# Attention by pairs of heads, first table rows beside the scores, values ahead of the gates in the combining

## The reference, cut to what matters

```python
def softmax_attend(q, k, v):
    s = jnp.einsum('bqhd,bkhd->bhqk', q, k).astype(jnp.float32) * MLA_SCALE
    p = jax.nn.softmax(s, axis=-1).astype(v.dtype)
    return jnp.einsum('bhqk,bkhd->bqhd', p, v)
...
def peer_ffn(h, wq, k1, k2, u, v):
    ...
    s1 = jnp.einsum('thd,kd->thk', q[..., :PEER_HALF], k1).astype(jnp.float32)
    s2 = jnp.einsum('thd,kd->thk', q[..., PEER_HALF:], k2).astype(jnp.float32)
    t1, i1 = lax.top_k(s1, PEER_TOPK)
    t2, i2 = lax.top_k(s2, PEER_TOPK)
    ...
        ue = jnp.take(u, ib, axis=0)
        ve = jnp.take(v, ib, axis=0)
        act = jax.nn.gelu(jnp.einsum('td,thkd->thk', hb, ue), approximate=False)
        return jnp.einsum('thk,thkd->td', gb * act, ve)
```

## Time and profile before

| | us |
|---|---|
| median of three executions (4664.24 to 4667.33) | 4665.28 |
| the profiled execution's own time | 4668.22 |
| its span, first to last instruction | 4666.4 |
| TensorE busy | 4111.4 (88%) |
| VectorE busy | 2964.6 (64%) |
| ScalarE busy | 1555.0 (33%) |
| GpSimd busy | 1471.2 (32%) |
| bytes moved | 1004.75 MB, 215 GB/s |

### The profile page before, as it was taken

How to read it: one execution, slowest core, us unless ns; L and a number is a source line. 1 busy time by engine, 2 the same in 40 slices (tenths; PEclk the granted TensorE clock), 3 DMA queues, 4 the chain that set the end, 5 groups by cost and what they waited for, 6 DMA issues and landing times. The chain is left out here.

```text
span 4666.4 us, 71661 instructions
## 1 busy us (share of the span) xinstructions
PE 4111.4 (88%) x23812; PEld 2234.3 (48%) x23812; DVE 2964.6 (64%) x8223; ACT 1555.0 (33%) x1960; POOL 1471.2 (32%) x1087
## 2 busy tenths in 40 slices
PE   5999779789999999699999996887888887789996
PEld 1556565556565566344444441443445454534442
DVE  2025544244664664688888886584188888688887
ACT  0014321024444444322222221681045443433332
POOL 0500000321111111166666650210512332277774
PEclk8989989899999999899999998898989998999998
DMA  5100221256877877699999984211388999999996
GB/s 213 58 24 4 75 73 72 82 133 165 242 196 186 235 190 200 211 370 338 350 338 350 339 310 167 77 59 59 109 226 265 338 314 323 326 337 344 345 343 226
DMA packets 374788, 1004.75 MB, mean 215 GB/s; under 512 B 35024, under 2 KB 121872, under 8 KB 367248
## 3 DMA queue, kind: packets, MB, share of 16 engines
q1 hardware_dynamic: 208188, 522.43, 32.4%
q0 software_dynamic: 101376, 318.81, 24.1%
q10 hardware_dynamic: 64996, 160.55, 9.2%
HBM read 804.43 MB, written 146.90 MB: 204 GB/s over the span
## 5 line engine op out<-in xcount | busy, mean ns | idle before, releaser
L1368 PE MATMUL ca_A<-hh,ca_uh 128*128 128x512 f16 (+2 forms) x3072 | 797.3, 314 | 135.1 <-DMA ca_ul<-ca_ur 72.2
L1368 PE MATMUL ca_A<-hl,ca_uh 128*128 128x512 f16 (+2 forms) x3072 | 796.9, 314 | 0.0
L1368 PE MATMUL ca_A<-hh,ca_ul 128*128 128x512 f16 (+2 forms) x3072 | 795.7, 314 | 0.0
L1332 POOL DMA_DIRECT2D ca_ul<-ca_ur x192 | 170.4, 887 | 1171.2 <-ACT ca_ul L1401 1109.7
L1874 PE MATMUL ex_R<-ex_vh,ex_wh 128*128 128x512 f16 x1280 | 486.4, 380 | 29.2 <-DVE ex_wl L1888 29.2
L1874 PE MATMUL ex_R<-ex_vl,ex_wh 128*128 128x512 f16 x1280 | 486.4, 380 | 0.0
L1874 PE MATMUL ex_R<-ex_vh,ex_wl 128*128 128x512 f16 x1280 | 486.1, 380 | 0.0
L1368 PEld LDWEIGHTS ca_A<-hh,ca_uh 128*128 128x128 f16 x3072 | 261.9, 99 | 329.7 <-issue 86.9
L1409 ACT ACTIVATE ca_ga<-ca_A 128x640 f32<-128x640 f32 (+1 forms) x256 | 152.7, 596 | 673.1 <-PE ca_A L1368 606.5
L1368 PEld LDWEIGHTS ca_A<-hh,ca_ul 128*128 128x128 f16 x3072 | 262.3, 99 | 196.5 <-issue 15.1
L1368 PEld LDWEIGHTS ca_A<-hl,ca_uh 128*128 128x128 f16 x3072 | 262.0, 99 | 190.8 <-issue 14.0
(11 more groups left out here) (374 smaller groups left out, 7767.5 us busy)
## 6 DMA issues: line engine op xcount, KB each, us to landing
ca_ur<-in_peer_u SPq DMA_DIRECT2D x256, 512.0 KB, 5.2
ex_vr<-in_peer_v SPq DMA_DIRECT2D x256, 512.0 KB, 7.5
gates<-ca_stage ACTq DMA_DIRECT2D x32, 2048.0 KB, 11.7
ca_ul<-ca_ur POOLq DMA_DIRECT2D x192, 256.0 KB, 5.2
acts<-ca_ga ACTq DMA_DIRECT2D x128, 320.0 KB, 2.6
ex_gr<-gates SPq DMA_DIRECT2D x32, 1280.0 KB, 7.8
ex_ar<-acts SPq DMA_DIRECT2D x128, 320.0 KB, 4.9
acts<-ca_ga ACTq DMA_DIRECT2D x128, 192.0 KB, 6.1
```

The lines of the kernel that those rows point to most:

```text
L1332: nc.gpsimd.dma_start(ul[j][:, :, :].rearrange("p k n -> p (k n)"), ur[j][:, :, :].rearrange("p k n -> p (k n)"), accum_op=ALU.add).then_i ...
L1368: last = nc.tensor.matmul(A[b][:, a:a + w], lhs[j][:, k, :], rhs[:, k, a:a + w], start=(k == 0 and x == 0), stop=(k == KD - 1 and x == 2))
```

## The change

In attention, the head's weights shrink to 3 x 128 columns for the queries and 2 x 64 for the keys; the values' weights of all heads are a tensor of their own, loaded once, and one token tile's values are made for all eight heads at once (two products of 512 columns, two tiles behind each of the first three pairs of heads). The keys of two heads are made by turns into rows 0 to 63 and 64 to 127 of `at_T`. The steps are numbered by pairs (`place`): two steps that follow are the two heads of a pair at the same tile. Their second products are made together, one step later than before, by turns into the two halves of one output; the copies of probabilities have four buffers, two of them in the space of the rotary turning, so ScalarE waits for `roped` first. VectorE copies the output of both at once, every second step.

The ring of the choosing, its semaphores among them, is made before the scores (`table_ring`) and cleared with a barrier behind the choosing. In the scores SyncE loads its first four chunks after all weights, and VectorE makes their high and low parts ahead of the last two score copies (`first_cut`). The choosing then begins with chunk 4 in its refills, and ScalarE, VectorE and GpSimd leave out their work on the first four chunks.

In both combining stages SyncE loads the four values of the first group first, then gates, then activations; ScalarE casts the values first; VectorE makes the first group's low parts of the values ahead of the weights; and GpSimd starts with the gathers. The second layer's (`combine_with_dots`) is changed as the first's, which is shown.

```diff
+        w = [sb(f"at_w{j}", [P, W_Q + W_K]) for j in range(2)]
+        wv = sb("at_wv", [P, 2, HEADS * V_DIM])
...
-        probT = [sb(f"at_pT{j}", [P, TOK]) for j in range(2)]
+        probT = [sb(f"at_pT{j}", [P, TOK]) for j in range(2)] + [rot[:, j, :] for j in range(2)]
...
-        C = ps("at_C", [P, TILES, V_DIM])
-        O0 = ps("at_O", [P, P])
-        O = (O0[0:64, :], C[0:64, 0:2, :].rearrange("p a d -> p (a d)"))
+        C = [ps(f"at_C{j}", [P, HEADS * V_DIM]) for j in range(2)]
+        O = [x[:, 0:P] for x in C]
...
+            def place(n):
+                m, s = divmod(n, 2)
+                g, i = divmod(m, TILES)
+                return 2 * g + s, i
+
+            keys = lambda n: CTX if place(n)[1] < CTX_TILES else TOK
...
+                    sp.dma_start(w[0][:, :], io["ev_w_up"][0]).then_inc(w_in[0], 16)
+                    sp.dma_start(w[1][:, :], io["ev_w_up"][1]).then_inc(w_in[1], 16)
                     sp.dma_start(cs[64:128, :], io["rope"]).then_inc(cs_in, 16)
-                    for h in range(1, HEADS):
-                        if h >= 2:
-                            sp.wait_ge(v_done, h - 1)
-                        sp.dma_start(w[h % 2][:, :, :], io["ev_w_up"][h].rearrange("p (k m) -> p k m", k=5)).then_inc(w_in[h % 2], 16)
+                    sp.dma_start(wv[:, :, :], io["ev_w_up_v"]).then_inc(wv_in, 16)
+                    for g in range(1, PAIRS):
+                        sp.wait_ge(k_done, g)
+                        for s in range(2):
+                            sp.dma_start(w[s][:, :], io["ev_w_up"][2 * g + s]).then_inc(w_in[s], 16)
...
+                    def key_pair(g):
+                        if g >= 1:
+                            pe.wait_ge(k_copied, 2 * g)
                         for a, n in HALVES:
                             for kk in range(2):
-                                last = nc.tensor.matmul(T[0:64, a:a + n], w[j][:, 3 + kk, 0:64], PT[:, C_KV + kk, a:a + n],
-                                                        start=(kk == 0), stop=(kk == 1))
+                                for s in range(2):
...
+                                    last = nc.tensor.matmul(T[64 * s:64 * s + 64, a:a + n], w[s][:, W_Q + kk * NOPE:W_Q + kk * NOPE + NOPE],
+                                                            PT[:, C_KV + kk, a:a + n], start=(kk == 0), stop=(kk == 1))
                         last.then_inc(k_done, 1)
...
+                    def values(t):
+                        if t >= 2:
+                            pe.wait_ge(v_copied, t - 1)
+                        for kk in range(2):
+                            last = nc.tensor.matmul(C[t % 2][:, :], PT[:, C_KV + kk, t * P:t * P + P], wv[:, kk, :],
+                                                    start=(kk == 0), stop=(kk == 1))
                         last.then_inc(v_done, 1)
...
+                    def mix_values(m):
+                        pe.wait_ge(pt_copied, 2 * m + 2)
+                        if m >= 2:
+                            pe.wait_ge(out_copied, m - 1)
+                        blocks = keys(2 * m) // P
+                        for b in range(blocks):
+                            for s in range(2):
+                                h, i = place(2 * m + s)
+                                last = nc.tensor.matmul(O[m % 2][64 * s:64 * s + 64, :], v[:, h, b, :],
+                                                        probT[(2 * m + s) % 4][:, b * P:b * P + P], start=(b == 0), stop=(b == blocks - 1))
+                        last.then_inc(av_done, 1)
+
+                    for g in range(PAIRS):
+                        queries(2 * g)
+                        queries(2 * g + 1)
+                        key_pair(g)
+                        if g == 0:
+                            pe.wait_ge(wv_in, 16)
+                        for t in range(2 * g, min(2 * g + 2, TILES)):
+                            values(t)
+                    pe.wait_ge(q_copied, HEADS)
+                    pe.wait_ge(k_copied, HEADS)
+                    pe.wait_ge(roped, HEADS)
+                    scores(0)
+                    scores(1)
+                    pe.wait_ge(v_copied, TILES)
+                    for n in range(STEPS):
+                        turn(n)
                         if n + 2 < STEPS:
                             scores(n + 2)
-                        pe.wait_ge(pt_copied, n + 1)
-                        if n >= 2:
-                            pe.wait_ge(out_copied, n - 1)
-                        for b in range(keys(n) // P):
-                            last = nc.tensor.matmul(O[n % 2], v[:, h, b, :], probT[n % 2][:, b * P:b * P + P],
-                                                    start=(b == 0), stop=(b == keys(n) // P - 1))
-                        last.then_inc(av_done, 1)
+                        if n >= 2 and n % 2 == 0:
+                            mix_values(n // 2 - 1)
+                    mix_values(STEPS // 2 - 1)
...
+                    for g in range(PAIRS):
+                        for s in range(2):
+                            h = 2 * g + s
+                            act.wait_ge(q_done, h + 1)
+                            nc.scalar.activation(q[0:64, h, :], A[s][0:64, 0:TOK], ACT.Copy).then_inc(q_copied, 1)
+                        act.wait_ge(k_done, g + 1)
+                        for s in range(2):
+                            nc.scalar.activation(k[2 * g + s][0:64, :], T[64 * s:64 * s + 64, 0:TOK], ACT.Copy).then_inc(k_copied, 1)
+                        for t in range(2 * g, min(2 * g + 2, TILES)):
+                            act.wait_ge(v_done, t + 1)
+                            nc.scalar.activation(v[:, :, t, :], C[t % 2][:, :].rearrange("p (h d) -> p h d", d=V_DIM), ACT.Copy).then_inc(v_copied, 1)
+                    act.wait_ge(roped, HEADS)
                     for n in range(STEPS + 1):
                         if n < STEPS:
...
-                            if o >= 2:
-                                act.wait_ge(av_done, o - 1)
-                            nc.scalar.activation(probT[o % 2][:, 0:keys(o)], T[:, 0:keys(o)], ACT.Copy).then_inc(pt_copied, 1)
+                            if o >= 4:
+                                act.wait_ge(av_done, o // 2 - 1)
+                            nc.scalar.activation(probT[o % 4][:, 0:keys(o)], T[:, 0:keys(o)], ACT.Copy).then_inc(pt_copied, 1)
...
+                        if n >= 4 and n % 2 == 0:
+                            m = n // 2 - 2
+                            g, i = divmod(m, TILES)
+                            dve.wait_ge(av_done, m + 1)
+                            nc.vector.tensor_copy(MIX[:, g, i * P:i * P + P], O[m % 2]).then_inc(out_copied, 1)
...
+@contextmanager
+def table_ring(nc, layer, leading):
+    with ExitStack() as c:
+        ring = lambda n, d: [c.enter_context(nc.sbuf_tensor(f"ca_{n}{b}{layer}", [P, KD, P], d)) for b in range(RING)]
+        ur, uh, ul = ring("ur", F32), ring("uh", F16), ring("ul", F16)
+        u_in0, u_in1, u_in2, u_in3, u_cut0, u_cut1, u_cut2, u_cut3, u_split, first_cut = c.enter_context(
+            signals(nc, "u_in0", "u_in1", "u_in2", "u_in3", "u_cut0", "u_cut1", "u_cut2", "u_cut3", "u_split", "first_cut"))
+        yield Ring(ur, uh, ul, (u_in0, u_in1, u_in2, u_in3), (u_cut0, u_cut1, u_cut2, u_cut3), u_split, first_cut,
+                   (True, False) * (RING // 2) if leading else (True,) * RING)
...
+                    for j in range(RING):
+                        sp.dma_start(ring.ur[j][:, :, :], io["peer_u"][layer][j].rearrange("p (k n) -> p k n", k=KD)).then_inc(ring.u_in[j], 16)
...
+                    def copy_scores(h):
                         for j in range(2):
                             dve.wait_ge(s_prod, h * 2 + (j + 3))
                             dve.wait_ge(stored[j], h * 16 + 16)
                             nc.vector.tensor_copy(so[j][:, :, :], S[j][:, 0:nt, :]).then_inc(s_copied, 1)
 
+                    with dve.Fori(0, PH - 1) as h:
+                        copy_scores(h)
+                    for j in range(RING):
+                        dve.wait_ge(ring.u_in[j], 16)
+                        nc.vector.tensor_copy(ring.uh[j][:, :, :], ring.ur[j][:, :, :]).then_inc(ring.u_split, ring.split[j])
+                    for j in range(RING):
+                        dve.wait_ge(ring.u_split, ring.split_upto[j])
+                        nc.vector.tensor_tensor(ring.ul[j][:, :, :], ring.ur[j][:, :, :], ring.uh[j][:, :, :],
+                                                ALU.subtract).then_inc(ring.first_cut, 1)
+                    copy_scores(PH - 1)
...
                     for j in range(RING):
-                        sp.dma_start(ur[j][:, :, :], u_src[j].rearrange("p (k n) -> p k n", k=KD)).then_inc(u_in[j], 16)
-                    with sp.Fori(1, PCH // RING) as k:
+                        sp.wait_ge(first_cut, j + 1)
```

(45 more changed lines are left out.)

161 lines of the change are left out of this document (77 added, 84 removed).

## The result

The changed kernel takes 4624.3 us (four runs, 4620.4 to 4627.2) against 4665.2 in the same comparison: a ratio of 0.9907 (0.9894 to 0.9920), 40.9 us less where 61.5 was forecast.

The account below looks back on a forecast made before the run. TensorE was taken to bound the choosing and combining, while in attention all engines take turns. The terms -45.9 - 14.2 - 7.3 + 0.8 + 5.1 = -61.5 from 4665.3 gave 4604 us, range 4586 to 4632.

Parts of the forecast that it names:

- Attention: Attention stage: projections minus 20.1 us and softmax minus 25.8, together minus 45.9; bounds minus 15 and minus 52.
- factor of two for column halves: Attention's paired products: the two column halves run at once, a factor of 2; bounds 1 and 2.7.
- A: Attention: the column halves do not overlap; loss 26.8 us, time 4631; chance 0.14.
- C: Attention: every change of column half empties the array, showing both weight loads; time 4702, slower; chance 0.05.
- softmax step: Attention: a step of 768 keys falls from 3.55 to 3.05 us, bound by VectorE's written order, not TensorE.
- The starts of the choosings: Both choosings: early table rows are ready at the start; first minus 14.2 us, second minus 7.3 (bounds minus 3, minus 10).
- Rival B: Choosings: early rows don't help, VectorE's splitting delays last copies or chunk 4 is late; loss up to 21.5, 4625; chance 0.08.
- In such a stage only TensorE's start can be moved: First choosing and combining: TensorE is nearly always busy (917.2 of 956.0 us in the choosing), so only its start can gain.
- Combining: Both combining stages: TensorE's first product comes later, plus 5.0 us in the first layer, plus 0.1 in the second.
- the collision with the gathers: Combining starts: early gathers share bandwidth with SP's loads; first layer's loads land at 1979.7, without collision at 1972.
- rival D: Combining: the gathers don't hinder the loads, so minus 7.1 us instead of plus 5.1, time 4592; chance 0.13.
- the ring: Choosings: the ring's own semaphores are cleared with a barrier after each; plus 0.4 us each, at most 1.

Follow-up runs that it names:

- the kernel with one block: Changed kernel, a pair's second product taking only the first 128 of its 256 or 768 keys: attention 186.2 us against 186.4, whole time 55.9 under before's.

## Why the prediction was right, and where it was not

**Attention** is the best-grounded part: -48.2 for -45.9. The factor of two for column halves, taken from the 0.094 us of the 64x64 tiles, held within 0.01 us; the Trainium skill's sentence that weight loads overlap only with another row group ("TensorE: Matmul & The Clock Gate", "Part 3: Packing small matmuls") is contradicted by loads and products that start 7 ns apart with only the column half changed, so rivals A and C are out. The softmax step was to take 3.05 and took 2.93: the chain from a maximum's start (405.13) to the end of normalizing (407.52 + 0.62) is 3.01 us as before, but the next maximum starts 0.08 before that end (408.06), where 0.04 had been added. In 32 steps that is 3.8 us; the whole stretch gained only 2.1 on the sum (129.4 for 131.5), which had, among smaller things, no term for the 4.1 us from the first score to the first transpose. That VectorE's order binds is shown by the kernel with one block.

**The starts of the choosings**: -13.6 for -14.2 in the first. In the second TensorE began 15.7 earlier and had kept 11.2 at the end, with 7.3 forecast; the second choosing's length varies between 662 and 675 us over the profiles, so no more can be read from it. Rival B is out: VectorE's eight instructions ended at 938.9, after which it waited 8.5 us for the last scores (2.1 in the second layer), and chunk 4 came without a wait in both.

**The step that failed** is "In such a stage only TensorE's start can be moved": I priced the choosing's start and put its other 900 us at nothing, since TensorE's loop does the same work. The work did not change, its place in the list did. Attention's list is 84 products and 24 waits shorter, and at each of the loop's three jumps back TensorE, whose code is fetched in 16384 bytes, ran dry a second time: +6.7 us of stalls (10.6 to 17.3). Its products themselves took 7.2 longer (924.4 against 917.2 us: the stage's length less all its waits), since behind a double pause it works longer at 1.2 GHz: a granted clock of 0.53 from 1203 to 1213 where the kernel before had 0.83 behind the same jump (1263 to 1273), two products in 0.53 instead of 0.27 us, and 0.98 over the whole stage against 0.99; the last 0.5 are other waits. This 14.4 is nearly all of what is missing in the sum. The Trainium skill has this rule ("Runtime: NRT & Kernel Launch", "Instruction fetch mechanics": code is refilled in blocks of 256 instructions, and a taken branch out of the window forces a fetch of the target's block); the runs agree, 128 products with their weight loads between transfers, and add that a target just before a block's end pays twice.

**Combining**: +6.9 for +5.4 in the first stage, the loads landing at 26.1 us instead of the 24.7 forecast; the collision with the gathers (not rival D) is shown by the run with later gathers. Of the two terms in it, the combining's own change costs 5 us against the kernels with the changed choosing alone, as forecast; the ring, priced at 0.4 with no row behind it, goes with some 2, and what in the changed choosing costs them is open. In the second stage I had left out two things: the last activations were stored 2.3 us later behind ScalarE (a wait of 16.9 for the store before, 14.6 in the kernel before), whose cause I have not tested, and SyncE's loads of the second group, issued only 3.1 us ahead of TensorE's first product (8.9 before), since the weights now come last; GpSimd's low parts were then 3.01 us late, +2.8; that the loads' late issue is why is argued, but with the combining as before the stage takes 535.7 to 537.1 us in seven profiles, and changed 539.7 to 541.7 in five. The start of this stage varies, with its code as before, from 32.8 to 35.3 us, and before's 32.8 is the lowest: a part of the +3.2 is chance.

Forecast and result differ by 20.6 us: 14.4 in the first choosing, 1.5 and 5.5 around the combinings, -2.3 and -3.9 where attention and the second choosing gave more, 0.6 at the first start, -0.2 elsewhere, and 5.0 between the profiled executions and their medians. The time stayed within the range by luck: the range had been stretched for rivals that did not come (4625 was rival B's price), and nothing in it stood for the loss in the first choosing.

## What to carry to other kernels

Before pricing an edit at nothing outside its own stage, count by how many instructions, waits included, it moves the loops behind it: a loop whose jump lands just before a block's end costs TensorE a second stall at each turn and then its clock, and a dozen small products in an idle place repaired it here. Heads of 64 columns are worth pairing in the two column halves, alternating product by product or by twos. Transfers that are issued early are not free while the stage's first loads are under way, but held back they come due later; a list's order should be changed only after its whole ring of waits has been walked.

## What the runs showed of the hardware

- Two products whose outputs lie in partitions 0 to 63 and 64 to 127 run at once with all 128 rows in use: 24 records of 128 columns in 1.53 us against 12 in 1.52; starts 7 ns apart. They need not alternate strictly: with a change after every second product of keys 16 records took 2.78 us to the next start instead of 2.73, and around one single change of half about eight records of 24 overlapped.
- TensorE fetches its code in 16384 bytes, some 128 records of products with their loads; waits take room in it too. At a jump back it stands still for 1.6 to 5.1 us, and in seven of the kernels' profiles a second time, 10 products later for 0.7 to 3.9 us or 22 later for 0.6 to 1.2. The first choosing takes 928 to 935 us without the second stalls, 942 to 950 with those after 10 products.
- 88 small records with 128x128 weights in float32 took 18.9 us, 0.21 each, although they stream eight columns; 64 records with 128x8 weights took 1.75 us and did not delay the stage.
